# Layer 1's attention: a score product of 289 rows laid as two passes of 128 rows and one of 33

## The reference, cut to what matters

```python
MLA_HEADS, MLA_NOPE, MLA_ROPE, MLA_V = 16, 64, 32, 64
MLA_QK = MLA_NOPE + MLA_ROPE                      # 96

def attn_core(q, k, v, scale):
    s = jnp.einsum('bqhd,bkhd->bhqk', q, k) * scale
    p = jax.nn.softmax(s, axis=-1)
    return jnp.einsum('bhqk,bkhe->bqhe', p, v)

def mla_mixer(a_lat, a_ctx, ...):                 # layer 1
    ...                                           # q: 1024 x 16 heads x 96, k: 1280 x 16 x 96, v: 1280 x 16 x 64
    o_l = sweep_query_blocks(lambda qi, kk, vv: attn_core(qi, kk, vv, scale), q_l, k_all, v_all)
    out_l = o_l.reshape(b, n, MLA_HEADS * MLA_V) @ w_out
```

## Time and profile before

| what | value |
|---|---|
| median of 3 runs | 3340.7 us (3339.87 to 3345.86) |
| span of the profiled execution | 3337.1 us |
| median over that span | 3.6 us |
| TensorE busy over the span | 3122.7 us, 94% |
| VectorE, GpSimd, ScalarE | 58%, 55%, 30% |
| layer 1's attention, core part | 1984 to 2540 us of the span |
| moved by DMA | 297.27 MB |

### The profile page before, as it was taken

How to read it: one execution, slowest core, us unless ns; L and a number is a source line. 1 busy time by engine, 2 the same in 40 slices (tenths; PEclk the granted TensorE clock), 3 DMA queues, 4 the chain that set the end, 5 groups by cost and what they waited for, 6 DMA issues and landing times. The chain is left out here.

```text
span 3337.1 us, 43882 instructions
## 1 busy us (share of the span) xinstructions
PE 3122.7 (94%) x14814; PEld 2566.5 (77%) x14814; DVE 1946.7 (58%) x2628; ACT 999.0 (30%) x1747; POOL 1819.9 (55%) x1681
## 2 busy tenths in 40 slices
PE   7997988999999999999898869999998999999999
PEld 6776776688888888888786747777776778888887
DVE  5584876654444444444536756677775775445454
ACT  4322665231000000000333436666664321001010
POOL 4683544443222222222433237777777788888885
PEclk9998989999999999999998969999998999999999
DMA  6367221512222222222123782323323211211112
GB/s 229 127 195 190 60 56 47 178 57 70 63 63 63 63 63 63 63 63 63 51 79 123 245 250 59 87 58 72 73 58 103 86 45 50 63 50 57 44 50 82
DMA packets 160194, 297.27 MB, mean 89 GB/s; under 512 B 53344, under 2 KB 98144, under 8 KB 159968
## 3 DMA queue, kind: packets, MB, share of 16 engines
q1 hardware_dynamic: 148576, 254.08, 25.4%
q10 hardware_dynamic: 11520, 41.95, 4.4%
HBM read 233.06 MB, written 62.91 MB: 89 GB/s over the span
## 5 line engine op out<-in xcount | busy, mean ns | idle before, releaser
L1390 POOL TENSOR_TENSOR a_pl<-a_p,a_ph 128x512 fp32r<-128x512 f32 x320 | 430.4, 1367 | 134.8 <-ACT a_p L1364 134.1
L2318 DVE SCALAR_TENSOR_TENSOR residual<-ps,mod,residual 128x512 f32<-128x512 f32 (+1 forms) x440 | 302.7, 696 | 309.7 <-PE ps L164 309.6
L164 PE MATMUL ps<-mixed_hi,l_whi 128*128 128x512 f32 (+1 forms) x1200 | 426.5, 355 | 5.9 <-PE ps L164 3.9
L128 POOL TENSOR_TENSOR small<-ident 128x1 f32<-128x1 f32 x108 | 42.0, 389 | 705.0 <-PE ps L164 405.7
L164 PE MATMUL ps<-mixed_lo,l_whi 128*128 128x512 f32 (+1 forms) x1200 | 425.4, 354 | 0.0
L164 PE MATMUL ps<-mixed_hi,l_wlo 128*128 128x512 f32 (+1 forms) x1200 | 425.1, 354 | 0.0
L164 PE MATMUL ps<-hidden,l_whi 128*128 128x512 f32 (+1 forms) x1056 | 284.2, 357 | 6.3 <-POOL l_wlo L139 5.1
L164 PE MATMUL ps<-a_q,a_k 97*128 97x512 f32 x960 | 270.1, 397 | 1.0 <-DVE a_q L1299 1.0
L164 PEld LDWEIGHTS ps<-mixed_hi,l_whi 128*128 128x128 f32 x1200 | 227.3, 189 | 39.8 <-issue 8.0
L164 PEld LDWEIGHTS ps<-mixed_hi,l_wlo 128*128 128x128 f32 x1200 | 227.1, 189 | 31.8
L164 PEld LDWEIGHTS ps<-mixed_lo,l_whi 128*128 128x128 f32 x1200 | 227.3, 189 | 31.4
(11 more groups left out here) (344 smaller groups left out, 7489.4 us busy)
## 6 DMA issues: line engine op xcount, KB each, us to landing
l_raw<-in_w_ffn SPq DMA_DIRECT2D x66, 512.0 KB, 3.6
raw<-in_w_ffn SPq DMA_DIRECT2D x66, 512.0 KB, 3.7
l_vraw<-in_mod_t ACTq DMA_DIRECT2D x48, 512.0 KB, 3.7
a_k<-scratch_k SPq DMA_DIRECT2D x32, 480.0 KB, 6.2
f_vraw<-in_mod_t ACTq DMA_DIRECT2D x24, 512.0 KB, 4.2
a_q<-scratch_q SPq DMA_DIRECT2D x32, 384.0 KB, 4.7
a_k<-scratch_k SPq DMA_DIRECT2D x32, 320.0 KB, 8.1
a_v<-scratch_v SPq DMA_DIRECT2D x32, 320.0 KB, 4.9
```

The lines of the kernel that those rows point to most:

```text
L128: e.nc.gpsimd.tensor_tensor(e.spare[:, 0:1], e.ident[:, 0:1], e.ident[:, 0:1], ALU.mult)
L164: last = nc.tensor.matmul(out, a, b, start=at == 0, stop=at == n - 1)
L1390: nc.gpsimd.tensor_tensor(pl[:, kk % 2, c], p[:, kk % 2, c], ph[:, kk % 2, c].bitcast(F32), ALU.subtract).then_inc(s["pl"], 1)
L2318: last = nc.vector.scalar_tensor_tensor(h[:, m, a:a + w], e.ps[:, o:o + w], e.mod[:, g, c:c + 1], h[:, m, a:a + w], ALU.mult, ALU.add)
```

## The change

The rows of a score product are laid out anew. Before, three products of 96 rows each (and a 97th row for the maximum) are three passes over the array. Now high q (96), low q (96) and high q again (96) stand on top of each other as 288 rows, facing high k, high k and low k, and with the row of the maximum they are 289: two passes of 128 rows and one of 33.

`q1` and `k1` are stored as (16, 192, ...), high rows then low rows of one head. `load` fills `ks` and `qs` to 128 rows from them, in pieces, and two new buffers: `kc` and `qc`, which hold the last 33 rows, for query half 0 in partitions 0 to 32 and for half 1 in partitions 64 to 96. All ten transfers of a head but the first two of head 0 count on `qk{par}`, and the first maximum product waits for them all. The 33rd row holds ones in `kc` (GpSimd, at the start) and minus the maximum in `qc` (VectorE). Both halves' passes of 33 rows are issued together, in `scores_rest`, behind the full passes of both halves and behind the second auxiliary unit; `st` is raised there, once for each half. The wait for the maximum's row (`auxr`) moves from the first scores of a head to `scores_rest`.

```diff
@@ store_turn
-                        to = dst[4 * u8:4 * u8 + 4, :, 256 * g:256 * g + 256].rearrange("(h x) d t -> x d h t", x=2)
-                        sp.dma_start(to[x, :, :, :], buf[:, n % OUTS, :].rearrange("p (h t) -> p h t", h=2).bitcast(F32))\
+                        to = dst[2 * u8:2 * u8 + 2, x * QK1:(x + 1) * QK1, 256 * g:256 * g + 256].rearrange("h d t -> d h t")
+                        sp.dma_start(to, buf[:, n % OUTS, :].rearrange("p (h t) -> p h t", h=2).bitcast(F32))\
@@ attention1
+        kc, qc = sb("a1_kc", [128, 2, T], F32R), sb("a1_qc", [128, 2, BANK], F32R)
@@ load
-                    for x in range(2):
-                        at = s["early"] if first and par == 0 and x == 0 else s[f"qk{par}"]
-                        sp.dma_start(qs[0:QK1, par, x, :].bitcast(F32), S["q1"][bass.ds(h * 2 + x, 1), :, :]
-                                     .rearrange("o p t -> p (o t)")).then_inc(at, 16)
-                        sp.dma_start(ks[0:QK1, par, x, :].bitcast(F32), S["k1"][bass.ds(h * 2 + x, 1), :, :]
-                                     .rearrange("o p t -> p (o t)")).then_inc(at, 16)
-                        if at is s["early"]:
-                            sp.wait_ge(at, 32)
+                    def part(dst, name, r0, rows, at, a=0, b=None):
+                        src = S[name][bass.ds(h, 1), r0:r0 + rows, a:b].rearrange("o p t -> p (o t)")
+                        sp.dma_start(dst.bitcast(F32), src).then_inc(at, 16)
+
+                    full = s[f"qk{par}"]
+                    early = s["early"] if first and par == 0 else full
+                    part(ks[:, par, 0, :], "k1", 0, 128, early)
+                    part(qs[0:QK1, par, 0, :], "q1", 0, QK1, early)
+                    if first and par == 0:
+                        sp.wait_ge(early, 32)
+                    part(qs[QK1:128, par, 0, :], "q1", 0, 32, full)
+                    part(qs[:, par, 1, :], "q1", 32, 128, full)
+                    part(ks[0:64, par, 1, :], "k1", 128, 64, full)
+                    part(ks[64:128, par, 1, :], "k1", 0, 64, full)
+                    for x in range(2):
+                        part(kc[64 * x:64 * x + 32, par, :], "k1", 64, 32, full)
+                        part(qc[64 * x:64 * x + 32, par, :], "q1", 160, 32, full, x * BANK, x * BANK + BANK)
@@ aux
-                            pe.wait_ge(s[f"qk{par}"], (g - par) * 32 + 64)
+                            pe.wait_ge(s[f"qk{par}"], (g - par) * 80 + 160)
@@ scores
-                    if kk == 0 and x == 0:
-                        pe.wait_ge(s["auxr"], h * AUX + AUX + 2)
-                    kh_, kl_ = (ks[0:QK1 + 1, par, x, kk * 128:(kk + 1) * 128] for x in range(2))
-                    qh_, ql_ = (qs[0:QK1 + 1, par, y, a:a + BANK] for y in range(2))
-                    products(nc, e.ps[:, o:o + BANK], [(kh_, kl_, qh_, ql_)]).then_inc(s["st"], 1)
+                    for y in range(2):
+                        nc.tensor.matmul(e.ps[:, o:o + BANK], ks[:, par, y, kk * 128:(kk + 1) * 128], qs[:, par, y, a:a + BANK],
+                                         start=y == 0, stop=False)
+
+                def scores_rest(h, par, kk):
+
+                    if kk == 0:
+                        pe.wait_ge(s["auxr"], h * AUX + AUX + 2)
+                    for x in range(2):
+                        o, r = (kk % 2) * 2 * BANK + x * BANK, slice(64 * x, 64 * x + 33)
+                        nc.tensor.matmul(e.ps[:, o:o + BANK], kc[r, par, kk * 128:(kk + 1) * 128], qc[r, par, :],
+                                         start=False, stop=True).then_inc(s["st"], 1)
@@ step of TensorE
+                    following = (h, par, kk + 1) if kk < KS - 1 else (h + 1, 1 - par, 0) if more else None
                     for x in range(2):
-                        if kk < KS - 1:
-                            scores(h, par, kk + 1, x)
-                        elif more:
-                            scores(h + 1, 1 - par, 0, x)
+                        if following:
+                            scores(*following, x)
                         for u in units[x:x + 1]:
                             aux(h + 1, 1 - par, u)
+                    if following:
+                        scores_rest(*following)
                     value(h, par, kk, 0)
@@ read_aux of VectorE
-                        nc.vector.tensor_copy(qs[QK1:QK1 + 1, par, 0, x * BANK:(x + 1) * BANK],
-                                              e.ps[QK1:QK1 + 1, bank:bank + BANK]).then_inc(s["auxr"], 1)
+                        r = slice(64 * x + 32, 64 * x + 33)
+                        nc.vector.tensor_copy(qc[r, par, :], e.ps[r, bank:bank + BANK]).then_inc(s["auxr"], 1)
@@ GpSimd, constant rows at the start
-                nc.gpsimd.memset(zeros, 0.0).then_inc(s["zero"], 1)
-                    for dst, one in ((ks[QK1:QK1 + 1, par, 0, :], 1.0), (ks[QK1:QK1 + 1, par, 1, :], 0.0), (qs[QK1:QK1 + 1, par, 1, :], 0.0)):
-                        nc.gpsimd.tensor_scalar(dst, zeros[:, 0:dst.shape[1]], one, 1.0, ALU.add, ALU.mult).then_inc(s["rows"], 1)
+                    for x in range(2):
+                        r = slice(64 * x + 32, 64 * x + 33)
+                        nc.gpsimd.tensor_scalar(kc[r, par, :], e.sel[r, 2:3].broadcast_to([1, T]), 1.0, 1.0, ALU.mult, ALU.mult)\
+                          .then_inc(s["rows"], 1)
@@ scratch
-            ("q1", (HEADS1 * 2, QK1, LAT), F32), ("k1", (HEADS1 * 2, QK1, T), F32),
+            ("q1", (HEADS1, 2 * QK1, LAT), F32), ("k1", (HEADS1, 2 * QK1, T), F32),
```

More of the change, by code:

```diff
@@ L1138, in attention1 @@
         ident = sb("a1_ident", [128, 128], F32R)
-        s = {x: sem("a1_" + x) for x in ("early", "unit", "zero", "qk0", "qk1", "v0", "v1", "rows", "aux", "auxr", "neg", "st", "exp", "pl",
+        kc, qc = sb("a1_kc", [128, 2, T], F32R), sb("a1_qc", [128, 2, BANK], F32R)
+        s = {x: sem("a1_" + x) for x in ("early", "unit", "qk0", "qk1", "v0", "v1", "rows", "aux", "auxr", "neg", "st", "exp", "pl",
                                          "pv", "raw", "rec", "whole", "ohi", "out", "x")}
@@ L1281, in _ @@
                     aux(0, 0, u, True)
-                pe.wait_ge(s["qk0"], 64)
-                pe.wait_ge(s["rows"], 8)
+                pe.wait_ge(s["qk0"], 160)
+                pe.wait_ge(s["rows"], 6)
                 for x in range(2):
                     scores(0, 0, 0, x)
+                scores_rest(0, 0, 0)
                 walk(pe, step)
@@ L1391, in step @@
                                                 ALU.subtract).then_inc(s["pl"], 1)
-                zeros = p[:].rearrange("p x t -> p (x t)")[QK1:QK1 + 1, :]
-                nc.gpsimd.memset(zeros, 0.0).then_inc(s["zero"], 1)
-                pool.wait_ge(s["zero"], 1)
                 for par in range(2):
-                    for dst, one in ((ks[QK1:QK1 + 1, par, 0, :], 1.0), (ks[QK1:QK1 + 1, par, 1, :], 0.0), (qs[QK1:QK1 + 1, par, 1, :], 0.0)):
-                        nc.gpsimd.tensor_scalar(dst, zeros[:, 0:dst.shape[1]], one, 1.0, ALU.add, ALU.mult).then_inc(s["rows"], 1)
-                    pool.wait_ge(s["rows"], 4 * par + 3)
+                    for x in range(2):
+                        r = slice(64 * x + 32, 64 * x + 33)
+                        nc.gpsimd.tensor_scalar(kc[r, par, :], e.sel[r, 2:3].broadcast_to([1, T]), 1.0, 1.0, ALU.mult, ALU.mult)\
+                          .then_inc(s["rows"], 1)
+                    pool.wait_ge(s["rows"], 3 * par + 2)
                     nc.gpsimd.tensor_scalar(vs[:, par, :, VD1:2 * VD1], e.sel[:, 2:2 + VD1].rearrange("p (o v) -> p o v", o=1)
                                             .broadcast_to([128, TT, VD1]), 1.0, 1.0, ALU.mult, ALU.mult).then_inc(s["rows"], 1)
-                    pool.wait_ge(s["rows"], 4 * par + 4)
+                    pool.wait_ge(s["rows"], 3 * par + 3)
                 walk(pool, step)
```

## The result

The changed kernel takes 3475.1 us, median of 4 runs (3466.8 to 3477.8), beside 3340.3 for the kernel before on the same chip (4 runs, 3339.6 to 3345.9). The ratio is 1.0395, with a 95% interval of 1.0381 to 1.0409: slower by about 135 us where 65 were forecast, and 3 us beyond the upper end of the range. The sign and the place were right; the forecast had about half of the size.

What follows compares the result with a forecast made beforehand. TensorE, busy 94% of 3337.1 us, bounded the kernel, with each head's load close behind. Fourteen late loads with clock loss (63 us), +2 start, -1.3 last stretch, +1.6 last head gave +65: 3406 us, range 3358 to 3472.

Steps and rivals of the forecast that it cites:

- The load: Before each head's first maximum product: ten transfers landing late, 13.7 us from issue to product, TensorE idle 4.7 us.
- the count: Load time summed by transfer from partition-dependent rates plus 2.0 us fixed: 13.2 us (11.8 to 15.1), against 8.35 before.
- the usual landing: Load before the change: 8.9 us taken as usual, between 8.35 in one head and 9.9 in one that waited.
- The clock: TensorE behind each late load: clock falls after the idle time, 1.4 us a head lost (0 to 1.7).
- The change of row tile: Score passes in each step: going between full passes and the 33-row tiles costs nothing, as with the value product's columns.
- product to issue: From a head's first maximum product to SP's next load issue: 24.3 us forecast, 25.6 measured before.
- each change of row tile drains: Rival, score steps: 0.32 us a step, 3457 us; 3518 with the weight load not covered either; chance 0.12.
- Two passes in one slot: Score steps: the two 33-row passes share one slot of 0.2315 us, so three-unit steps last 3.24 us.
- Start and end: First and last heads: head 1's load 2 us late, last stretch -1.3 us, last head +1.6 us.
- the late release: Last head: both halves' scores come free only at the pair, 2.96 us against 2.78 a step, costing 1.6 us.
- Slower: Whole kernel: late load with shared slot 0.55, two slots 0.20, drains 0.12; together 0.87.

Runs made afterwards that it cites:

- e1_early: The changed kernel, but the first maximum product waits only for high q and high k, the other eight transfers awaited by the next head's first scores: 3348.1 us, ratio 1.0027.
- e4_fill: The changed kernel with twenty passes whose results nobody reads ahead of the first maximum product's wait for the load: 3436.7 us, ratio 1.0287.
- e6_before_more: The kernel before with five more transfers per load, four into 32 partitions and one into 128, awaited but unused: 3399.5 us, ratio 1.0169.
- e10_vlate: The changed kernel with a head's two value transfers held back until all ten score transfers have landed: 3465.2 us, ratio 1.0375.
- e7_six: The changed kernel, the first maximum product waiting for six of ten transfers, the four narrow ones awaited by the scores: 3439.1 us, ratio 1.0289.
- e3_same: e1_early with both passes of 33 rows in one row tile, partitions 0 to 32: 3374.0 us, ratio 1.0108.
- e2_full: e1_early with each pass of 33 rows laid as a full-tile pass of 97, zeros in the other half's rows: 3329.7 us, ratio 0.9967.
- e9_mixed: e2_full's late order of last passes in heads with a successor, e8_order's early order in the last head: 3325.7 us, ratio 0.9956.
- e5_before_early: The kernel before, its first maximum product waiting only for high q and k, low parts awaited by the first scores: 3329.3 us, ratio 0.9972.
- e8_order: e2_full with the last pass of each half directly behind its full ones, the order of before: 3330.9 us, ratio 0.9975.

## Why the prediction was wrong

The three terms add up. Of the 9.6 us by which a head grew, 5.7 are the load against e1_early (13.66 - 7.99), or 4.5 against before (13.66 - 9.17); 3.4 the clock (30.81 - 27.42); and against the 25.64 of before the passes themselves are 27.42 - 25.64 = 1.8. 4.5 + 3.4 + 1.8 = 9.7.

- **The load (right, its close number in part by luck).** Forecast 13.7 us from issue to product, measured 13.66 (12.5 to 15.1), with a wait 14 times, 5.5 us each. e1_early, e4_fill and e6_before_more show it to be the largest part. The working under the sum was off in ways that cancelled. In e10_vlate's load the first transfer landed after 5.0 us, where the count had 2.0 + 1.61 = 3.6; the next five took 6.15, where it had 6.48; and the four narrow ones 2.55 (2.1 by e7_six), where it had 3.06, so their rate was 180 GB/s and not 150. That is 13.7 against the count's 13.2, and the 0.55 added for the usual landing made up the rest. And TensorE was ready 8.0 us after the issue (e1_early), not 9, so that the same landing made it wait 5.5 us and not 4.7.
- **The clock (right in kind, mis-sized).** Forecast 1.4 us a head (0 to 1.7), measured 3.4 (3.3 by e4_fill). The earlier trace rows showed 2.8 us at half clock behind a wait of 4.4 us; here 7.7 us of dense work ran at half behind a wait of 5.3. 18 slots of 0.43 instead of 0.23 lose 3.6 us, and 3.4 is what the sum should have had. This is 2.0 us x 14 = 28 of the 69 us between forecast and result. One stretch with one wait was too little to bound it by.
- **The change of row tile (the step that failed).** The prediction costed it at nothing, "because the value product already goes from a stationary operand of 128 columns to one of 64 and back". It costs 0.41 us a step (e1_early's timeline, e3_same, and e1_early against e2_full). The 64 columns were no measure for it: there the weights are still loaded ahead, and at the row tile they are not. The prediction called them a column tile, but the trace says only that 64 columns are active; no run shows whether the array is divided for them at all. In product to issue this is 27.42 against 24.3, 3.1 us a head: seven pairs and the entry of an eighth, 7 x 0.41 + 0.10 = 3.0. It is 43 us of the 69; with the clock's 28 these are 71, and the remaining terms, the start above all, came out 2 us lower than forecast. The rival "each change of row tile drains" had 0.12 of the chances, at 0.32 us a step without the weight load and 0.70 with it; 0.41 lies between them. The Trainium skill's rule (TensorEngine Tiling (Array Packing), Key Properties), that a change of tiling mode drains TensorE, was weighed by those columns and put aside. For row tiles these runs agree with it in that each change costs some 0.2 us and has no weight load ahead; the page gives no price.
- **Two passes in one slot (right).** Two passes of 33 rows in different row tiles take 0.50 us together, and in one tile 0.73 (e3_same). The Trainium skill (TensorE: Matmul & The Clock Gate, Part 3: Packing small matmuls), by which matmuls in different row groups start some 4 ns apart, is borne out: the median here is 3 ns. But a step was 3.65 us, not 3.24: what sharing gave (0.23) was less than what entering and leaving the tiles took (0.41). With all 15 passes in full tiles the step is 3.48.
- **Start and end.** Last head 31.05, forecast about 31. The start was 2 us by forecast, and the first copy of sums comes at 2021.60 against 2021.24, though this start moves by several us from one execution to another. The last head agrees only in the sum: of the 1.7 us, e2_full has 1.1 from the late release (30.49), the forecast had 1.6 for it and nothing for the tiles.
- **The chances.** Slower had 0.87, and slower it was. The range ended at 3472 since it took late load and draining tiles as alternatives; they happened together. Both at the forecast's own prices, 3406 + 51, and the clock at 3.4 would have been 3485.

## What to carry to other kernels

Count going into a row tile and back as nearly two slots and not as none (0.41 us here), whatever a change of columns costs: by these numbers a layout in row tiles pays only if it saves two slots or more for each such visit, and this one saved one. When a product waits for a load of many transfers, let it wait for those it reads, in counters of their own, and issue them first: this alone brought the loss from 135 us down to 9.5 (3348.1 beside 3338.6), and e9_mixed, which has it, is 0.44% faster than the kernel before (0.3 to 0.6%). A wait of some 5 us on TensorE costs the wait and again more than half of it in clock, so a stall priced by its length alone is priced too low.

## What the runs showed of the hardware

- A pass that follows a change of row tile starts together with its own weight load (2212.08 and 2212.51 in e1_early) and is 0.50 us long instead of 0.39; a second pass in the same tile has its weights loaded 0.23 us ahead (e3_same), and so has a pass of 64 columns behind one of 128, which costs nothing.
- After waits of 5.3 us the granted clock was 0.50, the lower of the two levels (1.2 GHz), for 7.7 us of work that never paused. With e4_fill's passes, which left waits of 2.8 us at the most, it stayed at 1.00 in 12 of 14 heads.
- Transfers into 32 partitions, alternating between partitions 0 to 31 and 64 to 95, took 2.55 us for 0.46 MB (180 GB/s), with windows of up to 246 GB/s, near those into 64, and of 96 and 23 GB/s at the end (e10_vlate).
- Left open: some 5 us by which e5_before_early, e8_order and e9_mixed are faster in the runs than their attention explains. e2_full has no such rest: 8.9 us in the runs, 8.6 in the attention.
